# GpSimd's subtraction of the weights' high halves, cut into pieces of two k-tiles outside the feed-forwards

## What is computed

```python
# first_block, twice
h = h + 0.5 * swiglu(rms_norm(h, ffn1_norm[l]), ffn1_w_gu[l], ffn1_w_down[l])
c_q, c_kv, k_pe, hq, hf, hi, hg, ga, gb = split_cols(rms_norm(h, mix_norm[l]) @ w_in[l], IN_SPLITS)
y_a = mla(c_q, c_kv, k_pe, ...) @ w_proj_attn[l]          # softmax attention, 8 heads
y_b = hgrn2(hq, hf, hi, hg, ...) @ w_proj_rec[l]          # gated linear recurrence, 4 heads
h = h + (sigmoid(ga) * y_a + sigmoid(gb) * y_b) @ w_out[l]
h = h + 0.5 * swiglu(rms_norm(h, ffn2_norm[l]), ffn2_w_gu[l], ffn2_w_down[l])
# second_block, once
u, q, k, v, qi, ki, wi, gates = split(rms(x) @ w_in)
y_ssm = s5(u)                                             # complex state space model, then a GLU
y_att = dsa(q, k, v, qi, ki, wi)                          # attention over the top 128 of the keys
x = x + (sigmoid(g_ssm) * (y_ssm @ w_proj_ssm) + sigmoid(g_att) * (y_att @ w_proj_attn)) @ w_out
x = x + (silu(h2 @ w_ffn_gate) * (h2 @ w_ffn_up)) @ w_ffn_down
```

## Time and profile before

| | |
|---|---|
| median of 3 runs | 3339.74 us (3338.99 to 3341.43) |
| the profiled execution | 3329.44 us, of which 3327.7 us lie in its span |
| PE busy in the span | 3256.0 us (98%), granted clock 0.992 of full speed |
| PE weight loads | 2941.0 us (88%) |
| DVE | 1357.0 us (41%) |
| POOL | 1278.4 us (38%) |
| ACT | 1038.9 us (31%) |
| DMA | mean 90 GB/s |

### The profile page before, as it was taken

The page is one execution under the profiler, slowest core; times in us unless marked ns, Lnnn a source line. Parts: engine busy times, 40 slices in busy tenths (PEclk is TensorE's granted clock), DMA queues, the critical chain, the costliest instruction groups (busy, mean ns, idle before and its releaser), DMA issues.

```text
span 3327.7 us, 54395 instructions
## 1 busy us (share of the span) xinstructions
PE 3256.0 (98%) x21512; PEld 2941.0 (88%) x21512; DVE 1357.0 (41%) x2158; ACT 1038.9 (31%) x1462; POOL 1278.4 (38%) x589
## 2 busy tenths in 40 slices
PE   8999999999999999999999999999999999999999
PEld 7999988899999999999998988788888776788887
DVE  4121353477531213221263367633235678642212
ACT  4222343322332224222243322332324344332222
POOL 3444432122444434444343222444455442244443
PEclk9999999999999999999999999999999999999999
DMA  4333322133333333333222223333333433233333
GB/s 133 90 89 94 90 72 52 39 93 114 95 91 94 89 90 93 89 89 95 84 74 73 52 70 121 95 95 107 94 93 92 99 99 122 58 94 95 95 95 95
DMA packets 544847, 298.71 MB, mean 90 GB/s; under 512 B 23280, under 2 KB 528624, under 8 KB 544560
## 3 DMA queue, kind: packets, MB, share of 16 engines
q1 hardware_dynamic: 514128, 258.77, 27.5%
q10 hardware_dynamic: 30560, 37.72, 3.5%
HBM read 278.36 MB, written 16.91 MB: 89 GB/s over the span
## 4 chain that ended last, share of the span: by engine, by line
PE 67%; issue 24%; POOL 6%; DVE 3%; ACTq 0%; ACT 0%; DMA 0%; POOLq 0%; DVEq 0%; SPq 0%
PE pair L600 38%; PE pair L598 27%; POOL wl L485 6%; ACTq L1354 0%; DVE negt L2003 0%; PE aux L627 0%; DVE top L2002 0%; DVE R L2098 0%; DVE S5P L2067 0%; PE aux L1003 0%; PE pair L944 0%; DMA raw<-w_uq 0%; PE aux L1004 0%; PE aux L994 0%; PE aux L696 0%
## 5 line engine op out<-in xcount | busy, mean ns | idle before, releaser
L485 POOL TENSOR_TENSOR wl<-raw,wh 128x1024 fp32r<-128x1024 f32 (+4 forms) x549 | 1220.0, 2224 | 2008.3 <-ACT wh L1047 2007.2
L1047 ACT ACTIVATE wh<-raw 128x1024 fp32r<-128x1024 f32 (+4 forms) x549 | 528.7, 964 | 478.3 <-DMA raw<-ffn_w_down 154.3
L1474 DVE TENSOR_TENSOR tmp<-pair,rstd 128x528 f32<-128x528 f32 (+1 forms) x222 | 155.7, 702 | 807.4 <-PE pair L600 500.7
L600 PE MATMUL pair<-xh,wh 128*128 128x264 f32 x3072 | 461.6, 289 | 19.3 <-DVE xl L1488 14.4
L600 PE MATMUL pair<-xl,wh 128*128 128x264 f32 x3072 | 446.8, 284 | 0.0
L600 PE MATMUL pair<-xh,wl 128*128 128x264 f32 x3072 | 440.6, 284 | 0.0
L600 PEld LDWEIGHTS pair<-xh,wh 128*128 128x128 f32 x3072 | 403.9, 190 | 28.1 <-ACT wh L1047 9.3
L600 PEld LDWEIGHTS pair<-xl,wh 128*128 128x128 f32 x3072 | 403.2, 189 | 0.0
L600 PEld LDWEIGHTS pair<-xh,wl 128*128 128x128 f32 x3072 | 400.1, 188 | 0.0
L1498 DVE SCALAR_TENSOR_TENSOR hT<-pair,hT 128x528 f32 (+3 forms) x144 | 100.9, 701 | 471.6 <-PE pair L600 272.8
L598 PE MATMUL pair<-xh,wh 128*128 128x512 f32 x1064 | 291.9, 402 | 0.0
(11 more groups left out here) (342 smaller groups left out, 3878.9 us busy)
## 6 DMA issues: line engine op xcount, KB each, us to landing
raw<-ffn_w_gu SPq DMA_DIRECT2D x176, 512.0 KB, 3.8
raw<-w_in SPq DMA_DIRECT2D x103, 512.0 KB, 3.9
raw<-ffn_w_down SPq DMA_DIRECT2D x64, 512.0 KB, 3.8
raw<-ffn_w_down SPq DMA_DIRECT2D x32, 384.0 KB, 3.3
raw<-w_out SPq DMA_DIRECT2D x24, 512.0 KB, 3.9
raw<-w_ffn_gate SPq DMA_DIRECT2D x22, 512.0 KB, 3.8
raw<-w_ffn_up SPq DMA_DIRECT2D x22, 512.0 KB, 3.8
gate_scratch<-gst ACTq DMA_DIRECT2D x32, 256.0 KB, 2.5
```

The lines of the kernel that those rows point to most:

```text
L485: nc.gpsimd.tensor_tensor(wl[:, k % SPL, 0:n], raw[:, k % SPL, 0:n], wh[:, k % SPL, 0:n].bitcast(F32), ALU.subtract).then_inc(S["split_don ...
L600: mm = nc.tensor.matmul(pp[:, h, 0:th], wk, x[:, kk, t0 + h * th:t0 + (h + 1) * th], start=first, stop=last)
L1047: nc.scalar.activation(wh[:, k % SPL, 0:n], raw[:, k % SPL, 0:n], ACT.Copy).then_inc(S["split_hi"], 1)
L1474: v.tensor_tensor(halves(dst, th), psum_pair(0 if alone else k, th), halves(scale, th), ALU.mult).then_inc(S["evacuated"], 1)
```

## The change

In the named stages the subtraction of one unit is issued as instructions of two k-tiles (256 elements in each of 128 partitions), one behind the other and without a wait between them; the last of them counts up `split_done`. A unit of eight k-tiles becomes four instructions, one of four k-tiles two. The feed-forwards and the stages C, UQ, UKV and HG keep one instruction per unit. Nothing else of the program changes.

```diff
-            def split(l, k, kt, i=0):
-                n = kt * P
+            def split(l, k, kt, i=0, kp=None):
+
+                kp = kt if kp is None else kp
                 pool.wait_ge(S["split_hi"], U(l, k, i) + 1)
-                nc.gpsimd.tensor_tensor(wl[:, k % SPL, 0:n], raw[:, k % SPL, 0:n], wh[:, k % SPL, 0:n].bitcast(F32),
-                                        ALU.subtract).then_inc(S["split_done"], 1)
+                for k0 in range(0, kt, kp):
+                    n = slice(k0 * P, (k0 + kp) * P)
+                    ins = nc.gpsimd.tensor_tensor(wl[:, k % SPL, n], raw[:, k % SPL, n], wh[:, k % SPL, n].bitcast(F32), ALU.subtract)
+                ins.then_inc(S["split_done"], 1)
...
-                run(l, U_GATE, [KD] * 4, 4)
-                run(l, U_PROJ, [4] * 4, 4)
-                run(l, U_WO, [KD] * 4, 2)
+                run(l, U_GATE, [KD] * 4, 4, 2)
+                run(l, U_PROJ, [4] * 4, 4, 2)
+                run(l, U_WO, [KD] * 4, 2, 2)
...
-                split(None, U_IN2 + j, KD)
+                split(None, U_IN2 + j, KD, kp=2)
...
-                split(None, U_GATE2 + g, KD)
-            run(None, U_GLU, [4] * 4, 1)
-            run(None, U_PROJ2, [4] * 4, 4)
-            run(None, U_WO2, [KD] * 4, 2)
+                split(None, U_GATE2 + g, KD, kp=2)
+            run(None, U_GLU, [4] * 4, 1, 2)
+            run(None, U_PROJ2, [4] * 4, 4, 2)
+            run(None, U_WO2, [KD] * 4, 2, 2)
```

More of the change, by code:

```diff
@@ L480, in _, with run @@
             pool.sem_inc(S["evacuated"], PAIRS)
-            def split(l, k, kt, i=0):
-                n = kt * P
+            def split(l, k, kt, i=0, kp=None):
+                kp = kt if kp is None else kp
                 pool.wait_ge(S["split_hi"], U(l, k, i) + 1)
-                nc.gpsimd.tensor_tensor(wl[:, k % SPL, 0:n], raw[:, k % SPL, 0:n], wh[:, k % SPL, 0:n].bitcast(F32),
-                                        ALU.subtract).then_inc(S["split_done"], 1)
-            def run(l, k, kts, turns):
+                for k0 in range(0, kt, kp):
+                    n = slice(k0 * P, (k0 + kp) * P)
+                    ins = nc.gpsimd.tensor_tensor(wl[:, k % SPL, n], raw[:, k % SPL, n], wh[:, k % SPL, n].bitcast(F32), ALU.subtract)
+                ins.then_inc(S["split_done"], 1)
+            def run(l, k, kts, turns, kp=None):
                 with pool.Fori(0, turns) as i:
                     for j in range(4):
-                        split(l, k + j, kts[j], i)
+                        split(l, k + j, kts[j], i, kp)
             def ffn(l, ub, beside=None):
@@ L563, in _ @@
             more(2, 3)
-            split(None, U_GATE2 + EARLY + 3, KD)
+            split(None, U_GATE2 + EARLY + 3, KD, kp=2)
             more(2, 4)
-            split(None, U_GATE2 + EARLY + 4, KD)
+            split(None, U_GATE2 + EARLY + 4, KD, kp=2)
             more(3, 9)
```

## The result

The changed kernel took 3315.47 us (median of 6 runs, 3312.42 to 3318.24) beside 3339.44 for the kernel before in the same comparison (6 runs): a ratio of 0.9931 [0.9918, 0.9944], 24.0 us faster. The forecast was 3329.8 with a range of 3319 to 3340, so it was wrong: right in direction, too small by 14 us, and outside its range. A second comparison gave 0.9932 [0.9919, 0.9946] for the same kernel.

The account below looks back on a forecast made before the run. PE was taken as the bound, waiting mostly for DVE steps held by POOL's subtractions. Waits -9.9, WO +1.5 and clock -1.5 made -9.9 us, from a median of 3339.74 to 3329.8; range 3319 to 3340.

Parts of the forecast that it names:

- What bounds the kernel: Whole program: PE is busy 98%; its waits are nearly all for DVE, held up to 2.1 us by POOL's subtraction.
- The price of a piece: POOL's cut units: 0.68 us from piece to piece, 2.77 us for eight k-tiles (0.38 more), 1.41 for four.
- Who gets in between: Between POOL's pieces: after each piece a waiting DVE instruction runs, and POOL loses about its length.
- rival B: POOL keeps the port between pieces, so each hold lasts a whole unit: 3344 us, or 3347 at wider spacing; chance 0.09.
- What goes, by place: PE's waits in recurrence, `al`, state space model, attention and L2123 shrink as DVE's holds shorten: 9.9 us gained.
- recurrence: Recurrence beside GATE in both layers: PE's waits for L1816 shrink, except at the last levels; 2.4 us gained.
- L2126: Second block, L2123 before the change: pieces let two of four held DVE steps come sooner; 0.7 us gained.
- WO: First WO unit at three places: POOL's pieces end later and PE waits 0.5 us more each, 1.5 us added.
- The clock: PE's stretches at the lower granted clock after waits: shorter waits spare 1.5 us, bounds 0 and about 8.
- Rival A: Pieces hold DVE again and again: half of the 9.9 us is gained, WO costs 2.6; 3337.3 us, chance 0.18.
- Rival C: PE gives back what it gains, waiting for ACT or a DMA to bring the next weights; 3336 us, chance 0.13.

Follow-up runs that it names:

- the two parts: Pieces only in the two layers, 4.1 us below the kernel before; pieces only in the second block, 19.9 us below it.

## Why the prediction was wrong, point by point

- **What bounds the kernel.** Right: DVE's steps held by POOL's subtraction, and through them PE.
- **The price of a piece.** Right: 0.68 us apart was forecast, 1.41 for a pair. A pair that no DVE step interrupted took 1.44 us in the profile after (line below); the mean of 850 ns above has DVE's turns in it.

```profile
862.22 1.44 POOL L488 TENSOR_TENSOR wl<-raw,wh 128x256 fp32r<-128x256 f32 x2 [0.69 <-ACT wh L1050]
```

- **Who gets in between.** Right, and rival B is out: L2070 ran between two of four pieces that have no wait between them. The rule of the Trainium skill behind it (GPSIMD Engine Reference, section Instruction dispatch: each core begins the next instruction when its own share of the last is done) did not keep a waiting DVE instruction out here: it was let in within one piece's length, 0.97 us with its own 0.69. That a hold lasts to the end of the piece that runs, and no longer, is shown by all four sizes: at its longest (2.62, 1.54, 0.97 and 0.97 us for whole units, four, two and one k-tile) this step ended 0.54 to 0.55 us after the end of the piece in which it had asked.
- **What goes, by place.** 9.9 forecast, 9.8 in the list of waits, 10.2 in span x clock. By term the largest misses are 0.4 us each (recurrence 2.0 for 2.4, L2126 1.1 for 0.7).
- **WO.** +1.5 forecast. In the list PE's three waits there are 3.6 us against 0.8 + 1.4 + 1.1 = 3.3, so +0.3, and with WO whole the time is the same. Too high, by about 1.
- **The clock.** This is the step that failed: "Bounds: 0 and about 8 us [...] I take 1.5." It is up to 12 by the column of the clock loss, and the kernel that only filled waits shows 10. The value was wrong even for the traced pair, whose clock loss fell by 7 (26.6 to 19.9, span x (1 - clock)); 1.5 was chosen between the bounds without a reason. The bound was wrong for another reason. It was read from the slow stretches of the one profiled execution, which had a clock of .992, and was then applied to a median 10.3 us above it. That gap stood in the sum and was carried over as a constant: "in runs the forecast is 3339.74 - 9.9". It was no constant: after the change the gap was 2.2 us. A typical run has .989, and the trace at .988 of the kernel with a whole second block shows what that is: 22.2 us of clock loss there in place of 10.2, beside waits for the same steps. It went away with the waits. The profiled pair differ by 16.2 us, the medians by 24.0: for the profiled execution the right terms would have been 9.8 and some 7, less a little for WO.
- **Rival A** (pieces hold again and again): out, L1818's, L1825's and L1827's longest durations in the profile after are 0.86, 0.92 and 0.85 us, and the gain did not halve. **Rival C** (gains given back to ACT or the DMAs): not at 3336; the two parts' gains add up.

What stays open: why the clock falls in some executions behind a wait of 1.5 us and in others not. The runs show only that it fell less once the waits of the second block were shortened or filled; in the layers, where 3 us of waits went, the clock loss in the traces stayed at 17 us.

## What to carry to other kernels

Compare the profiled execution with the median of its own kernel, in time and in granted clock, before you size anything by it: a gap between them is a cost that the profile doesn't show, and here 7.8 of the 24 us lay in it. A wait of TensorE of one to three microseconds can cost its length again in slow matmuls behind it (seven waits of 11 us in all were filled, and 10 us came back), so price waits by both, and try filling them with unread products: a few lines of that gave ten of 24 us without touching the cause. Where one engine's instructions hold another's, what counts is how long the ones are that run beside the critical chain; cutting those from 2.4 to 0.7 us was worth it here, to 0.45 it was not, and cutting the others gave nothing.

## What was not expected of the hardware

- The spread of a single-core kernel's times, 14 us over 51 runs, went with its granted clock: 3342.6 at .987 and 3331.9 at .991. Shortening waits in some 400 us of the program left 2 us between six runs (second block only) and 6 us between eleven (the changed kernel).
- A higher mean clock is no gain by itself: .993, .996 and .997 went with 3314.6, 3309.7 and 3310.7 us.
- POOL's instruction of 128, 256, 512 and 1024 elements in 128 partitions: the means were 541, 850, 1405 and 2419 ns in these kernels, DVE's turns included. Cutting a unit in four costs POOL an estimated 0.5 us (from the pair of 1.44 us: 2.9 in place of 2.4) and 0.9 us where DVE got in once (3.25 in place of 2.38).
